# Rounded parts and remainders in the second layer's weighted sum of values, remainders by GpSimd, next scores ahead of it

## The chip, the cores and the metric

The kernel runs on one core of one Trainium2 chip. A core has five engines that run their own instruction streams and meet at semaphores: TensorE (PE, matrix products into PSUM; its weight loads are shown as PEld), VectorE (DVE), ScalarE (ACT), GpSimd (POOL) and SyncE (SP, which here issues transfers). The metric is the time of one execution on the device in microseconds (us). Each kernel was run several times and the median counts.

## What is computed

A trunk of two decoder layers over 256 tokens of 2048 values, in float32. Layer 0 has stick-breaking attention, layer 1 sparse attention, in which each query takes the 64 best of the admissible keys by an index score; both are followed by a gated MLP with a short convolution. The change touches the second layer's attention, the last two of these lines, for 16 query heads in 4 groups that share keys and values:

```python
s = jnp.einsum('btgrd,btkgd->btgrk', qg, k_sel).astype(jnp.float32) * attn_scale
s = jnp.where(valid[:, :, None, None, :], s, -jnp.inf)
p = jax.nn.softmax(s, axis=-1)
o = jnp.einsum('btgrk,btkgd->btgrd', p.astype(v.dtype), v_sel)
...
return out @ w_o
```

The kernel gathers nothing: it adds a mask (selm) to the scores of all 256 keys, so that the keys not chosen get weight zero.

## The kernel before

Weights stream from memory in 771 pieces of 128 x 1024 numbers through a ring of four buffers (raw). For every piece ScalarE makes the rounded part (w_hi, type float32r, line 276) and VectorE the remainder raw - w_hi (w_lo, line 716). TensorE multiplies w_hi with the rounded parts and remainders of the activations side by side (512 columns) and w_lo with the rounded parts (256 columns). So a product in near full precision is made of three single-pass products. float32 operands without such a split go through TensorE at full precision, in more passes.

The order of work is written out by hand, engine by engine. A function block1 on each engine stands for one group of four pieces, e = 0 to 3, of the second layer's input projection; the small steps of attention hang on these e. The 16 heads are worked in 8 pairs, t = 0 to 7. Of a pair t, TensorE does scores(t) (queries by keys, added to the mask that ScalarE has seeded in PSUM banks 6 and 7 by seed_scores), VectorE maxes(t), ScalarE exps(t), VectorE normalise(t), TensorE transposes(t) of the 128 x 768 weights back into banks 6 and 7 behind piece e = 2, ScalarE prt_copy(t) to SBUF (prt, line 610) and then the seed for the next pair's scores (line 597), and TensorE values(t) behind piece e = 3: prt by v_cur, the values of the group, in full precision, with 512 and 256 columns. Behind it stands scores(t+1). ScalarE's out_hi(t) (line 617) and VectorE's out_lo(t) (line 1141) write the result as rounded part and remainder to att, and only then is att_ready raised. scores and values also wait for qr (VectorE, line 1052), the next queries.

Blocks 13 to 18 hold transposes and values of pairs 0 to 5, each with scores of the next pair. The last two pairs hang on the first group of the output projection (out_groups with l1_tail and l1_head; 8 pieces, e = 0 to 7): transposes(6) behind piece 1, values(6) and scores(7) behind piece 2, transposes(7) behind piece 4, values(7) behind piece 5. Piece e of this group multiplies the tiles of pair e, and wo1_ready(e) makes TensorE wait for att_ready of pair e. On ScalarE and VectorE each tail step stands behind the split of piece e + 4, which waits until TensorE has used piece e.

GpSimd fills three buffers at the start and issues three stores at the end of the second layer.

Of the kernel before, what the change touches and what calls it, by code (L numbers as in the profile page):

```python
# [81 lines left out]
def build(nc, x_in, w_all, vecs_in, consts_in, out):  # L82
    with ExitStack() as ctx:
# [3 lines left out]
        def sem(name):  # L87
            return ctx.enter_context(nc.semaphore(name))
# [41 lines left out]
        v_all = sb("v_all", [P, 2, 512], F32, l1)  # L130
        v_cur = sb("v_cur", [P, 2, P], F32, l1)
        k_all = sb("k_all", [P, KVH, T], F32, l1)
# [8 lines left out]
        score = sb("score", [P, 384], F32, l1)  # L141
        work = sb("work", [P, 384], F32, l1)
        cum = sb("cum", [P, 384], F32, l1)
        ones = sb("ones", [P, 256], F32, l1)
# [3 lines left out]
        cmask2 = sb("cmask2", [P, 384], F32, l1)  # L148
        tki = sb("tki", [P, 1, T], F32, l1)
        pr = sb("pr", [P, 2, 384], F32, l1)  # L150
        prt = sb("prt", [P, 2, 384], F32, l1)
        mx = sb("mx", [P, 2, 2], F32, l1)
# [37 lines left out]

        v1_ready, vcur_ready = sem("v1_ready"), sem("vcur_ready")
        tables_ready = sem("tables_ready")
# [8 lines left out]
        s_ready, mx_ready, nm_ready, p_ready, rc_ready, pn_ready = (sem(n) for n in ("s_ready", "mx_ready", "nm_ready", "p_ready", "rc_ready", "pn_ready"))  # L201
        tr_ready, pt_ready, av_ready = sem("tr_ready"), sem("pt_ready"), sem("av_ready")

# [13 lines left out]
        def f32(ap):  # L217
            return ap.bitcast(F32)

        def gain(m, tile):  # L220
# [34 lines left out]
        @block.gpsimd  # L255
        def _(pool):
            pool.memset(part[:, 0:2, :], 0.0).then_inc(warm_set, 1)
            pool.memset(upad[:, :, 0:2], 0.0).then_inc(pads_zero, 1)
            pool.memset(seed[:, 0:Z1], 0.0).then_inc(seed_zero, 1)

            for g in range(3):
                pool.wait_ge(x_ready, 12 + g + 1)
                pool.dma_start(out[:, 4 * g:4 * g + 4, :], xres[:, 4 * g:4 * g + 4, :]).then_inc(stored, 16)
            pool.wait_ge(stored, 48)
# [3 lines left out]
        def _(act):  # L268
# [339 lines left out]
            def prt_copy(t):  # L608
                act.wait_ge(tr_ready, t + 1)
                act.copy(prt[:, :, :], psum[:, 6:8, 0:384]).then_inc(pt_ready, 1)  # L610
                if not isinstance(t, int) or t < PAIRS - 1:
                    act.wait_ge(pt_ready, t + 1)
                    seed_scores()
# [5 lines left out]
            def set_v(g):  # L619

                act.copy(v_cur[:, :, :], v_all[:, :, bass.ds(g * P, P)]).then_inc(vcur_ready, 1)

# [67 lines left out]
            def l1_tail(e):  # L690
                if e == 1:
                    norm_scale(2, 10)
                    prt_copy(6)
                if e == 2:
                    out_hi(6)
                if e == 4:
                    prt_copy(7)
                if e == 5:
                    out_hi(7)
# [5 lines left out]
        def _(dve):  # L705
# [552 lines left out]
            def l1_tail(e):  # L1258
                if e == 0:
                    rope_prev(18, "q", 10, ("sin",))  # L1260
                if e == 2:
                    out_lo(6)
                if e == 5:
                    out_lo(7)
# [6 lines left out]
        def _(pe):  # L1271
# [294 lines left out]
            def values(t, n_v):  # L1566
                pe.wait_ge(pt_ready, t + 1)
                pe.wait_ge(vcur_ready, n_v)
                pe.wait_ge(att_ready, PAIRS + t)
                o = psum[:, 4, :].rearrange("p (h t) -> p h t", h=2)  # L1570
                mm(o, v_cur[:, 0, :], prt[:, :, 0:T], True)
                mm(o[:, :, P:T], v_cur[:, 1, :], prt[:, :, T:384]).then_inc(av_ready, 1)

            def block1(B, i, per, par, prev_nh, prev_nb, t_log, t_score, g_score, t_tr, n_v, base):
# [8 lines left out]
                for e in range(4):  # L1583
                    if index:
                        proj_index(base + e, i, per, 2 * par, 4 * e, e == 0)
                    else:
                        proj(base + e, i, per, 2 * par, xg, 4, 4 * e, 256, e == 0)
                    if e == 1 and prev_nb is not None:
                        mean_squares(prev_nh, prev_nb)
                    if e == 2 and isinstance(B, int) and B == 2:  # L1590
                        turn_wi()
                    if e == 2 and t_tr is not None:
                        transposes(t_tr)
                    if e == 3:
                        if t_log is not None:
                            logits(t_log)
                        if t_tr is not None:
                            values(t_tr, n_v)
                        if t_score is not None:
                            scores(t_score, g_score)  # L1600

# [29 lines left out]
            def l1_tail(e):  # L1631
                if e == 1:
                    mean_squares(2, 10)
                    transposes(6)
                if e == 2:
                    values(6, 4)
                    scores(7, 3)
                if e == 4:
                    transposes(7)
                if e == 5:  # L1640
                    values(7, 4)
# [88 lines left out]
```

## Time and profile before

| | |
|---|---|
| median of 3 runs | 2219.75 us |
| lowest and highest | 2219.74 and 2220.39 us |
| profiled execution | 2219.86 us |
| its span, first to last instruction | 2218.1 us |
| busy share: TensorE, VectorE, ScalarE, GpSimd | 100, 67, 53, 0% |
| granted clock of TensorE | 1.00 |

The profile shows one execution. The 2219.86 us contain the span and some 1.8 us around it. TensorE is busy all the time, so a timeline of its starts shows what each step costs; matmuls overlap, so the distance from one start to the next counts and not the duration printed, which reaches into the next. For the other engines a row in brackets says how long they sat idle and who ended it.

### The profile page before, as it was taken

To read this page: it belongs to the slowest core of one execution; us is meant where nothing else is said; L and a number is where in the kernel's file an instruction comes from. 1 tells how busy PE (TensorE), PEld (TensorE's weight loads), DVE (VectorE), ACT (ScalarE), POOL (GpSimd) and SP (SyncE) were. 2 spreads that over 40 slices of the span, in tenths; PEclk is the share of its full clock that TensorE was granted. 3 is DMA by queue.
4 is the path that set the end of the run, shared out by engine and by line. 5 is a ranking of instruction groups with operands and counts; after the bars stand their busy time and mean duration, and the time that the engine had idled before them with its cause. 6 is when DMAs were issued, how large, how long until landed. Compare 5 with 4: busy or idle time off the path is not lost. (4 is left out here: it accounts for less than half of the span.)

```text
span 2218.1 us, 35419 instructions
## 1 busy us (share of the span) xinstructions
PE 2211.4 (100%) x12790; PEld 1947.8 (88%) x12790; DVE 1494.5 (67%) x1774; ACT 1177.1 (53%) x1409; POOL 3.0 (0%) x10
## 2 busy tenths in 40 slices
PE   9999999999999999999999999999999999999999
PEld 8888898888888888888899888888888888888888
DVE  7666556677777777555578888667777777774444
ACT  7565555555555555444455466555555555553332
POOL 0000000000000000000000000000000000000000
PEclk9999999999999999999999999999999999999999
DMA  7555545555565555555566544455565656565654
GB/s 270 168 170 173 171 162 180 195 184 193 185 196 182 191 187 194 192 190 190 190 206 198 178 156 141 161 183 189 180 199 179 198 180 199 180 199 199 200 197 136
DMA packets 113686, 411.51 MB, mean 186 GB/s; under 512 B 12752, under 2 KB 13392, under 8 KB 113616
## 3 DMA queue, kind: packets, MB, share of 16 engines
q1 hardware_dynamic: 112608, 406.96, 55.9%
q10 hardware_dynamic: 576, 1.97, 0.2%
q0 software_dynamic: 432, 1.57, 0.2%
q8 instruction: 53, 0.87, 0.2%
q14 instruction: 17, 0.14, 0.0%
HBM read 408.36 MB, written 2.10 MB: 185 GB/s over the span
## 5 line engine op out<-in xcount | busy, mean ns | idle before, releaser
L716 DVE TENSOR_TENSOR w_lo<-raw,w_hi 128x1024 fp32r<-128x1024 f32 x769 | 935.2, 1224 | 670.9 <-ACT w_hi L276 665.1
L1273 PE MATMUL psum<-xg,w_hi 128*128 128x512 f32 (+1 forms) x3936 | 1358.5, 391 | 1.2 <-DVE xg L727 0.9
L276 ACT CAST w_hi<-raw 128x1024 fp32r<-128x1024 f32 x770 | 803.0, 1049 | 767.6 <-PE psum L1273 764.8
L1273 PE MATMUL psum<-xg,w_lo 128*128 128x256 f32 (+1 forms) x3920 | 1089.4, 278 | 0.0
L1273 PEld LDWEIGHTS psum<-xg,w_hi 128*128 128x128 f32 x3936 | 735.8, 187 | 156.6 <-issue 3.3
L1273 PEld LDWEIGHTS psum<-xg,w_lo 128*128 128x128 f32 x3920 | 741.2, 189 | 2.7 <-issue 2.2
L1273 PE MATMUL psum<-hid,w_hi 128*128 128x512 f32 x1408 | 488.2, 391 | 0.0
L1273 PE MATMUL psum<-hid,w_lo 128*128 128x256 f32 x1408 | 394.2, 280 | 0.0
L1273 PEld LDWEIGHTS psum<-hid,w_hi 128*128 128x128 f32 x1408 | 263.3, 187 | 57.7
L1273 PEld LDWEIGHTS psum<-hid,w_lo 128*128 128x128 f32 x1408 | 266.1, 189 | 0.0
L1273 PE MATMUL psum<-att,w_hi 128*128 128x512 f32 x512 | 178.8, 393 | 0.0
L976 DVE SCALAR_TENSOR_TENSOR conv<-upad,vecs,conv 128x256 f32<-128x256 f32 x352 | 147.0, 480 | 6.4
L1273 PE MATMUL psum<-att,w_lo 128*128 128x256 f32 x512 | 143.3, 280 | 0.0
L535 ACT ACTIVATE conv<-upad,vecs 128x256 f32<-128x256 f32 x176 | 91.6, 592 | 47.8 <-DVE upad L971 47.8
L1273 PEld LDWEIGHTS psum<-att,w_hi 128*128 128x128 f32 x512 | 95.8, 187 | 20.9
L1273 PE MATMUL psum<-w_hi,xg 128*128 128x512 f32 (+1 forms) x384 | 105.4, 357 | 0.0
L1273 PEld LDWEIGHTS psum<-att,w_lo 128*128 128x128 f32 x512 | 96.8, 189 | 0.1
L1273 PEld LDWEIGHTS psum<-w_hi,xg 128*128 128x128 f32 x384 | 68.3, 189 | 9.9
L1273 PE MATMUL psum<-w_lo,xg 128*128 128x512 f32 (+1 forms) x192 | 67.9, 354 | 0.0
L540 ACT ACTIVATE gates<-conv 128x1024 f32<-128x1024 f32 x22 | 23.4, 1062 | 72.4 <-DVE conv L976 72.4
L543 ACT CAST hid<-gates 128x1024 f32 x22 | 23.2, 1055 | 66.6 <-DVE gates L982 66.6
L971 DVE TENSOR_TENSOR upad<-part,rs 128x1024 f32<-128x1024 f32 x44 | 54.1, 1229 | 1.5
(166 smaller groups left out, 888.4 us busy)
## 6 DMA issues: line engine op xcount, KB each, us to landing
raw<-w_all SPq DMA_DIRECT2D x770, 512.0 KB, 3.4
xres<-x_in SPq DMA_DIRECT2D x3, 512.0 KB, 9.5
cst<-consts_in ACTq DMA_DIRECT2D x2, 768.0 KB, 6.0
out_t<-xres POOLq DMA_DIRECT2D x3, 512.0 KB, 3.7
raw<-w_all SPq DMA_DIRECT2D x2, 256.0 KB, 3.5
xres<-x_in SPq DMA_DIRECT2D x2, 256.0 KB, 4.5
out_t<-xres SPq DMA_DIRECT2D x4, 128.0 KB, 1.8
vecs<-vecs_in ACTq DMA_DIRECT2D x1, 354.0 KB, 7.9
```

The costliest lines, as they stand in the source:

```text
L276: act.copy(w_hi[:, c % RING, :], raw[:, c % RING, :]).then_inc(hi_ready, 1)
L535: last = act.activation(conv[:, k, :], upad[:, k, 0:T], ACT.Identity, scale=conv_scalars(layer, i, val, k, 0), bias=conv_scalars(layer, i, ...
L540: act.activation(gates[:, :, :], conv[:, :, :], ACT.Silu).then_inc(silu_ready, 1)
L543: act.copy(hid[:, bass.ds(4 * i, 4), 0:T], gates[:, :, :]).then_inc(h_hi, 1)
L716: dve.tensor_tensor(w_lo[:, c % RING, :], raw[:, c % RING, :], f32(w_hi[:, c % RING, :]), ALU.subtract).then_inc(lo_ready, 1)
L971: dve.tensor_tensor(upad[:, :, 2:T + 2], part[:, :, :], over_heads(rs[:, 0:T], 4), ALU.mult).then_inc(up_scaled, 1)
L976: last = dve.scalar_tensor_tensor(out=conv[:, k, :], in0=upad[:, k, j:j + T], scalar=conv_scalars(layer, i, val, k, j), in1=conv[:, k, :], ...
L1273: return pe.matmul(o, lhsT, rhs, start=start, stop=True, skip_group_check=True)
```

## The change

values(t) takes rounded parts and remainders. ScalarE copies the transposed weights twice, once in float32 (prt32) and once rounded (prt[:, 0]), and then raises pt_hi; GpSimd subtracts the one from the other (prt[:, 1]) and raises pt_ready. v_cur is made likewise, rounded by ScalarE, its remainder by GpSimd. TensorE makes three single-pass pairs of products in place of one pair in full precision. scores(t+1) stands ahead of values(t) everywhere. values(7), out_hi(7) and out_lo(7) move from behind piece 5 to behind piece 6. The seed waits for pt_hi. The buffers work, cum and tki of the key selection now lie in prt32.

```diff
@@ -257,6 +257,14 @@
+            for t in range(PAIRS):
+                if t % 2 == 0:
+                    g = t // 2
+                    pool.wait_ge(vcur_hi, g + 1)
+                    pool.tensor_tensor(v_cur[:, 1, :, :], v_all[:, :, g * P:(g + 1) * P], f32(v_cur[:, 0, :, :]), ALU.subtract).then_inc(vcur_ready, 1)
+                pool.wait_ge(pt_hi, t + 1)
+                pool.tensor_tensor(prt[:, 1, :, :], prt32[:, :, :], f32(prt[:, 0, :, :]), ALU.subtract).then_inc(pt_ready, 1)
@@ -607,9 +615,10 @@
             def prt_copy(t):
                 act.wait_ge(tr_ready, t + 1)
-                act.copy(prt[:, :, :], psum[:, 6:8, 0:384]).then_inc(pt_ready, 1)
+                act.copy(prt32[:, :, :], psum[:, 6:8, 0:384])
+                act.copy(prt[:, 0, :, :], psum[:, 6:8, 0:384]).then_inc(pt_hi, 1)
                 if not isinstance(t, int) or t < PAIRS - 1:
-                    act.wait_ge(pt_ready, t + 1)
+                    act.wait_ge(pt_hi, t + 1)
                     seed_scores()
@@ -618,7 +627,7 @@
-                act.copy(v_cur[:, :, :], v_all[:, :, bass.ds(g * P, P)]).then_inc(vcur_ready, 1)
+                act.copy(v_cur[:, 0, :, :], v_all[:, :, bass.ds(g * P, P)]).then_inc(vcur_hi, 1)
@@ -695,7 +704,7 @@
                 if e == 4:
                     prt_copy(7)
-                if e == 5:
+                if e == 6:
                     out_hi(7)
@@ -1260,7 +1269,7 @@
-                if e == 5:
+                if e == 6:
                     out_lo(7)
@@ -1568,8 +1577,11 @@
                 o = psum[:, 4, :].rearrange("p (h t) -> p h t", h=2)
-                mm(o, v_cur[:, 0, :], prt[:, :, 0:T], True)
-                mm(o[:, :, P:T], v_cur[:, 1, :], prt[:, :, T:384]).then_inc(av_ready, 1)
+                for hl in range(2):
+                    mm(o, v_cur[:, 0, 0, :], prt[:, hl, :, 0:T], hl == 0)
+                    mm(o[:, :, P:T], v_cur[:, 0, 1, :], prt[:, hl, :, T:384])
+                mm(o, v_cur[:, 1, 0, :], prt[:, 0, :, 0:T])
+                mm(o[:, :, P:T], v_cur[:, 1, 1, :], prt[:, 0, :, T:384]).then_inc(av_ready, 1)
@@ -1594,10 +1606,10 @@
+                        if t_score is not None:
+                            scores(t_score, g_score)
                         if t_tr is not None:
                             values(t_tr, n_v)
-                        if t_score is not None:
-                            scores(t_score, g_score)
@@ -1633,11 +1645,11 @@
                 if e == 2:
+                    scores(7, 3)
                     values(6, 4)
-                    scores(7, 3)
                 if e == 4:
                     transposes(7)
-                if e == 5:
+                if e == 6:
                     values(7, 4)
```

On TensorE, the end of a block with values and scores, before:

```order
L1273 MATMUL psum<-xg,w_lo 128x256
L1569 REGISTER_ALU [waits vcur_ready,pt_ready]
L1273 MATMUL psum<-prt,v_cur 128x512 [waits att_ready]
L1273 MATMUL psum<-prt,v_cur 128x2x128
L1550 REGISTER_ALU
L1551 REGISTER_ALU [waits qr_ready]
L1273 ISA [waits s_seeded]
L1273 MATMUL psum<-k_all,qr 128x128
L1273 MATMUL psum<-k_all,qr 128x256
```

The same place after:

```order
L1559 REGISTER_ALU
L1560 REGISTER_ALU [waits qr_ready]
L1282 ISA [waits s_seeded]
L1282 MATMUL psum<-k_all,qr 128x128
L1282 MATMUL psum<-k_all,qr 128x256
...
L1578 REGISTER_ALU [waits vcur_ready,pt_ready]
L1282 MATMUL psum<-prt,v_cur 128x512 [waits att_ready]
L1282 MATMUL psum<-prt,v_cur 128x2x128
```

The wait for the seed (s_seeded) now comes straight behind the piece, and the wait for the remainders (pt_ready) behind the scores.

On ScalarE, the same block, the split of piece e = 2 and what follows it, before:

```order
L276 CAST w_hi<-raw 128x1024 [waits piece_used]
L610 COPY prt<-psum 128x768 [waits tr_ready]
L597 COPY psum<-selm 128x2x384 [waits pt_ready]
L275 REGISTER_ALU [waits raw_full2]
L276 CAST w_hi<-raw 128x1024 [waits piece_used]
```

And after:

```order
L284 CAST w_hi<-raw 128x1024 [waits piece_used]
L618 COPY prt<-psum 128x768 [waits tr_ready]
L619 CAST prt<-psum 128x768
L605 COPY psum<-selm 128x2x384 [waits pt_hi]
L283 REGISTER_ALU [waits raw_full2]
L284 CAST w_hi<-raw 128x1024 [waits piece_used]
```

One 768-wide instruction more stands between the transposed weights and the seed.

On TensorE in the output projection's first group, at values(7), before (the last matmuls of piece 5, values, the first of piece 6):

```order
L1273 MATMUL psum<-att,w_hi 128x512
L1273 MATMUL psum<-att,w_lo 128x256
L1273 MATMUL psum<-prt,v_cur 128x512 [waits att_ready,vcur_ready,pt_ready]
L1273 MATMUL psum<-prt,v_cur 128x2x128
L1273 MATMUL psum<-att,w_hi 128x512 [waits lo_ready,att_ready]
```

After, with the last matmuls of piece 6, values (three such pairs in all) and then the first of piece 7:

```order
L1282 MATMUL psum<-att,w_hi 128x512
L1282 MATMUL psum<-att,w_lo 128x256
L1282 MATMUL psum<-prt,v_cur 128x512 [waits att_ready,vcur_ready,pt_ready]
L1282 MATMUL psum<-prt,v_cur 128x2x128
...
L1282 MATMUL psum<-att,w_hi 128x512 [waits lo_ready,att_ready]
```

The matmul behind values(7) that waits for att_ready is now that of piece 7, which needs the tiles of pair 7 itself.

## Rows read from the trace of the kernel before

**Rows 1.** The page, part 1; span and clock; longest wait of TensorE (total, times, longest).
```profile
PE 2211.4 (100%) x12790; PEld 1947.8 (88%) x12790; DVE 1494.5 (67%) x1774; ACT 1177.1 (53%) x1409; POOL 3.0 (0%) x10
...
core 0: 2218.1 us, clock 1.000
...
PE psum L1273 <- POOL part L257: 1.3, 1, 1.3
```
**Rows 2.** Timeline, TensorE, block 14: start, us, instruction; transposes(1), piece, values(1), scores(2).
```profile
1318.75 0.82 PE L1562 MATMUL psum<-cst,pr 128*128 128x128 f32 x6
1319.32 0.48 PE L1273 MATMUL psum<-xg,w_hi 128*128 128x512 f32 x1
...
1320.10 0.40 PE L1273 MATMUL psum<-xg,w_hi 128*128 128x512 f32 x1
1320.33 0.28 PE L1273 MATMUL psum<-xg,w_lo 128*128 128x256 f32 x1
1320.45 0.40 PE L1273 MATMUL psum<-xg,w_hi 128*128 128x512 f32 x1
...
1322.22 1.45 PE L1273 MATMUL psum<-prt,v_cur 128*128 128x512 f32 x4
1323.51 1.47 PE L1273 MATMUL psum<-k_all,qr 128*128 x8
1324.63 0.58 PE L1273 MATMUL psum<-xg,w_hi 128*128 128x512 f32 x1
1325.05 0.27 PE L1273 MATMUL psum<-xg,w_lo 128*128 128x256 f32 x1
```
**Rows 3.** Timeline, ScalarE, the same block.
```profile
1319.90 0.80 ACT L610 COPY prt<-psum 128x768 f32<-128x768 f32 x1
1320.72 0.80 ACT L597 COPY psum<-selm 128x768 f32<-128x768 f32 x1
1322.42 1.04 ACT L276 CAST w_hi<-raw 128x1024 fp32r<-128x1024 f32 x1 [0.89 <-PE psum L1273]
```
**Rows 4.** Timeline, VectorE, the same block.
```profile
1321.23 1.22 DVE L716 TENSOR_TENSOR w_lo<-raw,w_hi 128x1024 fp32r<-128x1024 f32 x1
1323.50 1.23 DVE L716 TENSOR_TENSOR w_lo<-raw,w_hi 128x1024 fp32r<-128x1024 f32 x1 [1.05 <-ACT w_hi L276]
```
**Rows 5.** First layer: ScalarE timeline, VectorE group; GpSimd groups (busy, mean ns).
```profile
63.35 0.84 ACT L349 CAST aw_hl<-aw 128x768 fp32r<-128x768 f32 x1
64.09 0.80 ACT L351 COPY psum<-seed 128x768 f32<-128x768 f32 x1
...
L814 DVE TENSOR_TENSOR aw_hl<-aw,aw_hl 128x768 fp32r<-128x768 f32 x7 | 6.7, 955 | 1.1 <-ACT aw_hl L349 1.1
...
L259 POOL MEMSET seed<- 128x512 f32 x1 | 0.5, 524 | 0.0
L1723 POOL MEMSET const-float32-1.0<- 128x1 f32 x1 | 0.1, 98 | 0.0
```
**Rows 6.** Timeline, TensorE, tail: piece 2; transposes(7); values(7) and piece 6.
```profile
1392.91 0.47 PE L1273 MATMUL psum<-att,w_hi 128*128 128x512 f32 x1
...
1403.92 0.82 PE L1562 MATMUL psum<-cst,pr 128*128 128x128 f32 x6
...
1407.40 1.45 PE L1273 MATMUL psum<-prt,v_cur 128*128 128x512 f32 x4
1408.50 0.59 PE L1273 MATMUL psum<-att,w_hi 128*128 128x512 f32 x1
1408.92 0.28 PE L1273 MATMUL psum<-att,w_lo 128*128 128x256 f32 x1
```
**Rows 7.** Timeline, ScalarE, tail: prt_copy(6), seed; split, out_hi(7).
```profile
1393.93 0.79 ACT L610 COPY prt<-psum 128x768 f32<-128x768 f32 x1
1394.75 0.80 ACT L597 COPY psum<-selm 128x768 f32<-128x768 f32 x1
...
1407.65 1.04 ACT L276 CAST w_hi<-raw 128x1024 fp32r<-128x1024 f32 x1 [1.73 <-PE psum L1273]
1408.89 0.59 ACT L617 CAST att<-psum 128x512 fp32r<-128x512 f32 x1 [0.19 <-PE psum L1273]
```
**Rows 8.** Timeline, VectorE, tail: qr, splits, out_lo(6), normalise(7), split, out_lo(7).
```profile
1395.28 0.69 DVE L1052 TENSOR_TENSOR qr<-ra,rsn 128x512 f32<-128x512 f32 x1
1395.89 2.44 DVE L716 TENSOR_TENSOR w_lo<-raw,w_hi 128x1024 fp32r<-128x1024 f32 x2
1398.24 0.68 DVE L1141 TENSOR_TENSOR att<-psum,att 128x512 fp32r<-128x512 f32 x1
...
1402.07 1.01 DVE L1135 TENSOR_SCALAR pr<-pr,rc 128x128 f32<-128x128 f32 x4
...
1408.73 1.22 DVE L716 TENSOR_TENSOR w_lo<-raw,w_hi 128x1024 fp32r<-128x1024 f32 x1 [2.25 <-ACT w_hi L276]
1409.87 0.68 DVE L1141 TENSOR_TENSOR att<-psum,att 128x512 fp32r<-128x512 f32 x1
```

More of the change, by code:

```diff
@@ L130, in build @@
         v_all = sb("v_all", [P, 2, 512], F32, l1)
-        v_cur = sb("v_cur", [P, 2, P], F32, l1)
+        v_cur = sb("v_cur", [P, 2, 2, P], F32R, l1)
         k_all = sb("k_all", [P, KVH, T], F32, l1)
@@ L141, in build @@
         score = sb("score", [P, 384], F32, l1)
-        work = sb("work", [P, 384], F32, l1)
-        cum = sb("cum", [P, 384], F32, l1)
         ones = sb("ones", [P, 256], F32, l1)
@@ L148, in build @@
         cmask2 = sb("cmask2", [P, 384], F32, l1)
-        tki = sb("tki", [P, 1, T], F32, l1)
         pr = sb("pr", [P, 2, 384], F32, l1)
-        prt = sb("prt", [P, 2, 384], F32, l1)
+        prt32 = sb("prt32", [P, 2, 384], F32, l1)
+        prt = sb("prt", [P, 2, 2, 384], F32R, l1)
         mx = sb("mx", [P, 2, 2], F32, l1)
@@ L189, in build @@
         att_hi, att_ready = sem("att_hi"), sem("att_ready")
-        v1_ready, vcur_ready = sem("v1_ready"), sem("vcur_ready")
+        v1_ready, vcur_hi, vcur_ready = sem("v1_ready"), sem("vcur_hi"), sem("vcur_ready")
         tables_ready = sem("tables_ready")
@@ L201, in build @@
         s_ready, mx_ready, nm_ready, p_ready, rc_ready, pn_ready = (sem(n) for n in ("s_ready", "mx_ready", "nm_ready", "p_ready", "rc_ready", "pn_ready"))
-        tr_ready, pt_ready, av_ready = sem("tr_ready"), sem("pt_ready"), sem("av_ready")
+        tr_ready, pt_hi, pt_ready, av_ready = sem("tr_ready"), sem("pt_hi"), sem("pt_ready"), sem("av_ready")
         wg = w_all.rearrange("n p k -> p n k")
@@ L218, in f32 @@
             return ap.bitcast(F32)
+        work, cum, tki = prt32[:, 0, :], prt32[:, 1, :], prt32[:, 0:1, 0:T]
         def gain(m, tile):
```

## The prediction, made before the kernel after was run

> **What bounds the kernel now.** The page's first part and the granted clock come first: TensorE is busy 100% of the span, at full clock throughout, VectorE 67%, ScalarE 53%, GpSimd not at all [rows 1]. A microsecond counts only where it lengthens or shortens TensorE's own row of work, so the change is read off TensorE's timeline at the eight places where a weighted sum of values is computed, here called values(0) to values(7). All times are starts from the timeline of one execution, whose matmul ends are modelled; I use start-to-start distances.
>
> Call P the first matmul of the weight piece that stands between transposes(1) and values(1): P = 1319.32 [rows 2]. The piece takes until P+2.90, values(1) 1.29 us (1322.22 to 1323.51), scores(2) 1.12 us (to 1324.63). The first matmul behind these full-precision ones occupies 0.42 us until the next start, where the same form elsewhere takes 0.23: 0.19 us, one weight load, is exposed there [rows 2]. Nothing else waits. values(0) to values(5) stand in six such blocks; values(6) has scores(7) behind it, values(7) stands alone.
>
> **TensorE's work.** A full-precision pair of 512 and 256 columns costs 1.29 us. In rounded form one pair costs 0.35 (1320.10 to 1320.45, or 1322.22 less 1319.32 over eight pairs with the first a little long) [rows 2]. Three pairs are 1.04. In the new order scores come first, the 0.19 falls at the head of values, and the following piece starts without it: 1.12 + 0.19 + 1.04 = 2.35 against 1.29 + 1.12 + 0.19 = 2.60. Gain 0.25. At values(7), 1.10 + 0.19 [rows 6] becomes 1.04: 0.25 too. **Eight times 0.25: -2.0 us.**
>
> **ScalarE's second copy and the scores put ahead.** ScalarE takes the transposed weights at P+0.58 and seeds the scores' banks from P+1.40 to P+2.20 [rows 3]. Now scores need that seed at P+2.90, where they had 1.29 us more. The second copy adds about 0.74, the distance between two 768-wide ScalarE instructions in a row (63.35 to 64.09) [rows 5]. The seed ends at P+2.94, and since the wait also exposes the scores' weight load (0.19) and a hand-over (0.05), scores start at P+3.15. **Six times 0.25: +1.5 us.** ScalarE's own next instruction stands at P+3.10 after 0.89 us idle [rows 3], so nothing behind the copy moves. In the last group ScalarE comes later: the piece starts at 1392.91, the copy at +1.02, the seed ends at +2.64 [rows 6, 7], now +3.38; scores(7) start at +3.60 and not +2.86: **+0.74 us.**
>
> **GpSimd's subtraction, the unknown term.** The rounded weights are out at P + 0.58 + 0.71 + 0.80 = P+2.09. Values could start at 3.15 + 1.12 + 0.19 = P+4.46, so the remainders must be there at P+4.22: GpSimd has 2.1 us. No row shows GpSimd with an operand to read. Its fills take 0.524 us for 512 columns and 0.098 for one [rows 5], 0.83 ns a column for one stream. For 768 columns one stream gives 0.74 us, two 1.37, and three (two reads, one write, nothing overlapped) 2.0. VectorE does it in 0.955 [rows 5]. I take 1.7, midway between two and three streams: two reads and a write on an engine that shows one stream at 0.83 ns a column, while VectorE, overlapping all three, needs 1.24. When does it start? VectorE runs its 1024-wide subtraction from P+1.91 to P+3.13, then idles 1.05 us [rows 4]. If both engines can read at once: done at P+3.85, no wait. If GpSimd has to let VectorE end: 3.13 + 1.7 = P+4.83, and values wait 0.6. Ends: -0 (one stream, 3.87 even from the late start) and 0.9 (three streams from the late start). It cannot be below zero, since nothing in the term shortens TensorE's row. I take the late start: the spare time of 0.4 us in the early case is used up by any hand-over, while VectorE is inside such an instruction at P+2.1 in every block. **Six times 0.6: +3.6 us.** VectorE's next conversion (P+4.18) is held to P+4.83 likewise, but the next block begins 0.6 later, so its phase stays.
>
> The Trainium skill bears on this. "SBUF — State Buffer", section "Who interferes with whom", says that a VectorE instruction with two SBUF inputs and a GpSimd instruction that reads SBUF exclude each other for their whole length, the first in going first. "GPSIMD Engine Reference", section 3.1, gives 2.6 cycles at 1.2 GHz for each element of such an operation: an estimate of 1.66 us here. By these the wait would be 0.56 us, without the exclusion none. No row of before can show either.
>
> **The tail.** values(6): the rounded weights are out at 1392.91 + 2.53; VectorE is in its 0.69 us multiply until +3.06 and then in two conversions until +5.42 [rows 8]. If GpSimd comes in between, it ends at +4.76, and values(6) start +0.1 late; behind both conversions it would be 2.4. I take **+0.1**. Then ScalarE's and VectorE's writing of values(6) comes late: before, VectorE's att subtraction starts at +5.33 and the weights of pair 7 are normalised at 1403.08 [rows 8], 0.84 before transposes(7) at 1403.92 [rows 6]. Now values(6) end at +6.0, ScalarE's cast follows at about +6.15 to +6.75, VectorE's subtraction at +6.76, 1.43 later; TensorE has slipped 0.5 only. 1.43 - 0.50 - 0.84 is 0.1 over, with an exposed load 0.3; with the held conversions another 0.3. **+0.6 us.** (0.3 of it belongs to GpSimd.)
>
> **One piece later for values(7).** Before, they stand between pieces 5 and 6 of the output projection. Piece 7 multiplies the very tiles that they produce. From the end of piece 5 (1407.40): ScalarE's conversion of the next weights from +0.25, its cast of the result from +1.49, VectorE's conversion from +1.33 to +2.55, its subtraction done at +3.15 [rows 6, 7, 8]. Piece 6 covered that (values(7) 1.10, piece 2.78: 3.9, so 0.7 to spare). Now values(7) stand behind piece 6. The chain is the same, since VectorE's conversion and not the values holds it: done at +3.15, the first matmul of piece 7 at +3.40 with hand-over and load, while TensorE is free at +1.04. **+2.36 us.** The cover, a piece of 2.78 us, is gone and nothing takes its place. The piece gained ahead of values(7) is not needed: remainders are ready about 1408.6 against 1410.2.
>
> The four small value subtractions (256 wide) have over 8 us before their first use; cost nothing, likewise the renamed buffers.
>
> **Sum:** -2.0 + 1.5 + 0.74 + 3.6 + 0.1 + 0.6 + 2.36 = +6.9 us. The profiled execution took 2219.86 us (span 2218.1), 0.1 over the median of three, so about 2226.8.
>
> **Rivals.**
> B, GpSimd is in time: it reads beside VectorE, or is faster than I take it. The 3.6, the 0.1 and 0.3 of the 0.6 go: +2.9, 2222.8. That is no measurable slowdown; it decides at an end of the subtraction before P+4.22. For it speaks that 2.1 us are more than two streams need. Chance 0.27.
> C, the stalls at the seed and at piece 7 are not there either, as they come from sums of 0.2 us hand-overs: only the -2.0, 2217.9. Against it stands the 2.36, where the cover misses by more than 2 us. 0.03.
> D, GpSimd loses to VectorE's back-to-back conversions: in block 0, where they run to P+3.85, and behind both in the tail, with pair 7 following: with three streams 2.9 + 5.4 + 0.7 + 4.8 = 13.8, thus 2233.7. Or TensorE's idle time of over 2 us ahead of piece 7 takes its clock from 2.4 to 1.2 GHz for a stretch: in this trace the level never falls, and TensorE's longest wait is 1.3 us [rows 1]. 0.08.
> E, rounded matmuls from these buffers cost more than a single pass, or what else I overlooked: 0.02.
>
> **The numbers.** The forecast case has 0.60: 2225 to 2231. With its neighbours the range goes from 2221.8 (B less 1 us of errors in the tail) to 2232.5. A measurement of this kernel can tell 0.2%, 4.4 us, from no change. B and C lie within it: 0.29 with a sliver of the forecast's low end. Slower 0.69. Faster by 4.4 us has no mechanism: 0.02.
>
> **What would show it.** In TensorE's timeline of after: scores at P+3.15 and not P+2.90; the first value matmul at P+5.05 (A) or P+4.46 (B); six value matmuls in 1.04 us; a gap of 2.4 us ahead of the last piece of the first output group. In GpSimd's rows: a subtraction of 1.7 us that begins when VectorE's conversion ends, and VectorE's next conversion held. Wrong would be: GpSimd's rows begin at P+2.1 and end before P+4.2, or a gap ahead of piece 7 under 1 us.

## The result

The changed kernel takes 2229.94 us in the median of five runs (2228.6 to 2230.65), the kernel before 2219.75 (2219.31 to 2220.39): 1.0046 times as long, 95% interval 1.0035 to 1.0056, or 10.2 us more. The profiled execution took 2230.65 us with a span of 2228.9; the spans differ by 10.8 us.

The page's first part and the span's clock answer to [rows 1]: GpSimd now works 24.5 us, and the clock is no longer 1.000.

```profile
PE 2216.9 (99%) x12806; PEld 1950.0 (87%) x12806; DVE 1501.3 (67%) x1774; ACT 1183.2 (53%) x1417; POOL 24.5 (1%) x22
...
core 0: 2228.9 us, clock 0.999
```

TensorE's waits from 1300 us on after the change (engine and line waited for: total us, times, longest). The kernel before has none there; its waits, like the other ones after the change, lie ahead of 1200 us:

```profile
PE psum L1282 <- DVE att L1150: 2.0, 1, 2.0
PE psum L1282 <- DVE qr L1061: 1.7, 1, 1.7
PE psum L1282 <- POOL prt L267: 1.3, 4, 0.4
PE psum L1282 <- ACT psum L605: 0.5, 1, 0.5
```

The last one is scores(7) waiting for the seed. They come to 5.5 us. The list leaves out pieces of idle time that a modelled matmul end covers, so the cost is better read from starts.

**A usual block.** TensorE's timeline of block 15 after the change (start, length, operation) answers to [rows 2] one block on: the piece's start P = 1336.83, scores(3), values(2), the next piece.

```profile
1336.83 0.48 PE L1282 MATMUL psum<-xg,w_hi 128*128 128x512 f32 x1
...
1339.88 1.57 PE L1282 MATMUL psum<-k_all,qr 128*128 x8
1341.87 1.32 PE L1282 MATMUL psum<-prt,v_cur 128*128 128x512 f32 x6 [0.41 <-POOL prt L267]
1343.03 0.39 PE L1282 MATMUL psum<-xg,w_hi 128*128 128x512 f32 x1
```

ScalarE's timeline there has the rounded cast, as [rows 3] had the copy:

```profile
1338.10 0.81 ACT L619 CAST prt<-psum 128x768 fp32r<-128x768 f32 x1
```

GpSimd's has the subtraction:

```profile
1338.99 2.66 POOL L267 TENSOR_TENSOR prt<-prt 128x768 fp32r<-128x768 f32 x1 [9.24 <-ACT prt L619]
```

And VectorE's the two conversions of [rows 4]:

```profile
1338.75 1.22 DVE L725 TENSOR_TENSOR w_lo<-raw,w_hi 128x1024 fp32r<-128x1024 f32 x1
1341.01 1.71 DVE L725 TENSOR_TENSOR w_lo<-raw,w_hi 128x1024 fp32r<-128x1024 f32 x1 [1.04 <-ACT w_hi L284]
```

GpSimd is asked at P+2.16 and shows 2.66 us, of which the first 0.98 lie inside VectorE's conversion (until P+3.14). It ends at P+4.82. VectorE's next conversion is asked at P+4.18 and shows 1.71 us in place of 1.23: it ends 1.07 after GpSimd. Each is stretched by about its overlap with the other: GpSimd by 0.83 over the 1.83 us that it takes alone (overlap 0.98), VectorE by 0.48 (overlap 0.64). Scores start at P+3.05, values at P+5.04 and the next piece at P+6.20, where 5.31 + 0.19 = 5.50 stood before: 0.70 us more.

**Block 14.** Here GpSimd came first. P = 1319.84. GpSimd's timeline, then VectorE's, then TensorE's, all after the change:

```profile
1321.99 1.83 POOL L267 TENSOR_TENSOR prt<-prt 128x768 fp32r<-128x768 f32 x1 [13.29 <-ACT prt L619]
```

```profile
1322.08 2.29 DVE L1061 TENSOR_TENSOR qr<-ra,rsn 128x512 f32<-128x512 f32 x1
```

```profile
1324.61 1.57 PE L1282 MATMUL psum<-k_all,qr 128*128 x8 [1.70 <-DVE qr L1061]
...
1327.07 0.39 PE L1282 MATMUL psum<-xg,w_hi 128*128 128x512 f32 x1
```

VectorE's query multiply, a 0.69 us instruction before, began 0.09 us after GpSimd and lasted 2.29. Scores need its result and started at P+4.77. This block lost 1.73 us.

**Piece 7.** values(7) begin at 1415.81. VectorE's timeline has the remainder of their result at its end:

```profile
1417.14 1.22 DVE L725 TENSOR_TENSOR w_lo<-raw,w_hi 128x1024 fp32r<-128x1024 f32 x1 [1.60 <-ACT w_hi L284]
1418.29 0.68 DVE L1150 TENSOR_TENSOR att<-psum,att 128x512 fp32r<-128x512 f32 x1
```

TensorE's has the first matmuls of piece 7, and two of those behind:

```profile
1419.03 0.50 PE L1282 MATMUL psum<-att,w_hi 128*128 128x512 f32 x1 [2.00 <-DVE att L1150]
...
1421.00 0.63 PE L1282 MATMUL psum<-att,w_hi 128*128 128x512 f32 x1
...
1421.64 0.63 PE L1282 MATMUL psum<-att,w_hi 128*128 128x512 f32 x1
```

Before, in [rows 6, 8], the piece followed without a break. A pair takes 0.64 us and not 0.35 between about 1420 and 1423.4. A view by stretches (TensorE busy, weight loads, VectorE, ScalarE, GpSimd, granted clock, DMA share, GB/s) shows the clock of that time:

```profile
1416.00:1419.00 3.00, 1.03 (x6) 0.61 (x5) 1.83 (x2) 1.58 (x2) 0.00 (x0) 1.00 0.55 175
1419.00:1424.00 5.00, 4.97 (x19) 4.25 (x20) 0.00 (x0) 0.26 (x1) 0.00 (x0) 0.66 0.30 105
1424.00:1430.00 6.00, 6.00 (x35) 5.20 (x35) 4.72 (x4) 4.28 (x7) 0.00 (x0) 1.00 0.27 87
```

A mean of 0.66 over five microseconds is some 3.4 us at the lower of the two levels, 1.2 GHz, and the rest at 2.4.

**The account of the 10.8 us**, from the same marks in both traces: 0.2 before the attention's blocks; 0.3 + 1.7 + 0.7 + 0.6 + 0.6 + 0.6 = 4.5 in blocks 13 to 18; 0.5 at scores(7) and values(6); 0.3 from there to piece 5; 2.1 at values(7) and piece 7; 1.6 for the clock; 1.3 in the three further groups of the output projection (22.61 us each against 22.19, see the end); 0.3 in all that follows, nearly all of it at the same slower pace.

### The profile page after: what moved, and what is told of

Its sections match the earlier page's. It is cut to its first block and busy times, and to the rows that moved or that the text cites. A ratio compares the mean times of both kernels' runs of the same rounds, so it can differ in the third digit from the quotient of the medians.

```text
span 2228.9 us, 35473 instructions
## 1 busy us (share of the span) xinstructions
PE 2216.9 (99%) x12806; PEld 1950.0 (87%) x12806; DVE 1501.3 (67%) x1774; ACT 1183.2 (53%) x1417; POOL 24.5 (1%) x22
## 3 DMA queue, kind: packets, MB, share of 16 engines
q10 hardware_dynamic: 576, 1.97, 0.2%
```

## The experiments

Medians are to be compared with 2229.94 for the changed kernel and 2219.75 to 2219.99 for the one before, which ran beside each of them. Ratios are to that one.

### values(7) back behind piece 5

```diff
-                if e == 6:
+                if e == 5:
                     out_hi(7)
...
-                if e == 6:
+                if e == 5:
                     out_lo(7)
...
-                if e == 6:
+                if e == 5:
                     values(7, 4)
```

> The changed kernel with values(7), out_hi(7) and out_lo(7) back behind piece 5 of the output projection. Theory (piece 7 waited 2.0 us for pair 7's result, and the 1.6 us at half clock behind it came from that idle time): both go, but values(7) now wait for GpSimd's remainders, which came 1.18 us after the end of piece 5 in the changed kernel (1412.07 + 1.85 + 0.24 against 1412.98). Sum -2.2 - 1.6 + 1.2 = -2.6 us: 2227.3. No wait ahead of piece 7, no stretch at half clock. Rival (the half clock has another cause, or any wait of 1 us brings it): the clock still falls, 2229 or more. Rival 2 (the piece-7 wait was not what it costs but was covered later): no change, 2229.9.

2226.22 us (1.0028, 1.0017 to 1.0038), 3.7 less than the changed kernel; 2.6 were expected. The wait for att and the stretch at half clock are gone, and GpSimd is waited for once more: values(7) started 3.88 us behind the start of piece 5, 0.98 late. TensorE's waits of this kernel:

```profile
PE psum L1282 <- POOL prt L267: 2.3, 5, 0.8
```

This idle time of 0.8 us left the clock at 1.00. Between the two profiled executions the order by itself makes 1.2 us, where 1.0 was expected (2.2 less 1.2), and the low stretch 1.6. The groups behind took 22.19 us and not 22.61, which makes another 1.5 us with what follows them and was in no expectation.

### Remainders by VectorE

```diff
+            def prt_lo(t):
+                dve.wait_ge(pt_hi, t + 1)
+                dve.tensor_tensor(prt[:, 1, :, :], prt32[:, :, :], f32(prt[:, 0, :, :]), ALU.subtract).then_inc(pt_ready, 1)
...
+                    if e == 3 and t_soft is not None:
+                        prt_lo(t_soft)
                     split(base + e + RING, i, per)
...
+                if e in (1, 4):
+                    prt_lo(6 + e // 4)
```

GpSimd's subtraction for prt is taken out; values(7) stay behind piece 6.

> The changed kernel with the remainders of the transposed weights made by VectorE instead of GpSimd, in the place where VectorE idled 1.04 us ahead of the split of piece e = 3 (tail: behind the split of pieces 1 and 4). Theory (GpSimd and VectorE hold each other up): the waits of values for GpSimd and the late qr of block 14 go, the six blocks lose 0.3, 1.7, 0.7, 0.6, 0.6, 0.6 us less, 4.5 together: 2225.4. VectorE's 0.96 us fits its idle time. Rival (VectorE is nearly full in these blocks, so that its own 0.96 us comes back as late queries or late conversions): gain under 2 us, 2228 to 2230. Piece 7 still waits 2.0 us and the clock falls in both.

2225.37 us (1.0025, 1.0015 to 1.0035): 4.6 less, 4.5 expected. That they agree so well is in part luck: the granted clock of a whole execution is 0.999 in four of the changed kernel's five and in one of this one's nine, so the medians compare a kernel that mostly has the low stretch with one that mostly has not. The two profiled executions both have it. In them, from block 13 to piece 2 of the output projection, the changed kernel loses 4.6 us on the one before and this one 0.8: GpSimd's part there is 3.8 us. VectorE has room for it, as its timeline of block 15 shows (P = 1335.35): conversion, remainder, conversion, with 0.20 us idle left of the 1.05.

```profile
1337.21 1.22 DVE L723 TENSOR_TENSOR w_lo<-raw,w_hi 128x1024 fp32r<-128x1024 f32 x1
1338.34 0.95 DVE L1147 TENSOR_TENSOR prt<-prt 128x768 fp32r<-128x768 f32 x1
1339.49 1.23 DVE L723 TENSOR_TENSOR w_lo<-raw,w_hi 128x1024 fp32r<-128x1024 f32 x1 [0.20 <-ACT w_hi L282]
```

Values now start at P+4.28, before the P+4.46 of the forecast, and the next piece at P+5.52, where it stood at 5.50 before. Blocks 14 to 18 lose 0.1 us in all; block 13 keeps 0.65, of which 0.3 are a wait for VectorE's remainder. The wait of 2.0 us ahead of piece 7 stays, and in the profiled execution a low stretch behind it that costs 1.4 us.

### Both

> Both edits of the two kernels before it. Theory: -4.5 for GpSimd, -2.2 and -1.6 for piece 7 and the clock, +0.4 since values(7) wait shortly for VectorE: about 2222, still 2 us over the kernel before, of which 1.5 + 0.7 are the seed's waits less the 2.0 that the single-pass products save. Rival (slow pace of products behind the waits is a cost of its own): up to 1.3 us less again, if it goes with the waits, 2220.7.

2223.18 us (1.0014, 1.0004 to 1.0023). The sum came out 1.2 higher than expected and the rival's 2220.7 is off by 2.5. With neither GpSimd nor the wait at piece 7, the kernel is still 3.3 us over the one before, in the profiled spans too. Of these, 0.8 stand in the blocks, nearly all in block 13, 1.0 at scores(7) and values(6), where the seed comes late and values start late behind the scores, and 1.5 in the pace of the later groups. That pace is the slow one here, with the long waits gone, so it does not go with them.

### Filling the gap ahead of piece 7

```diff
                 if e == 6:
                     values(7, 4)
+                    for n in range(6):
+                        mm(psum[:, 5, :], xg[:, 0, 0:P], xg[:, 1, :], True)
```

These products go to a bank that nobody reads.

> The changed kernel with six 512-wide rounded matmuls into an unused PSUM bank behind values(7), 1.3 us of the 2.0 us in which TensorE waits for pair 7. Theory (idle time took the clock down): piece 7 begins at the same time, the stretch at half clock is gone or shorter: -1.6 us, 2228.3. Rival (the half clock is not from that gap): unchanged 2229.9. If the filling itself delayed piece 7, its start would show it.

2228.64 us (1.0039), 1.3 less than without them; the profiled spans differ by 1.9, of which 0.3 came before this place. Piece 7 started 3.21 us behind values(7), as before (3.22), after a wait of 0.6 us. The view by stretches, as above, of this kernel:

```profile
1419.00:1424.00 5.00, 5.00 (x30) 4.30 (x29) 1.01 (x1) 1.96 (x2) 0.00 (x0) 1.00 0.34 105
```

Thirty matmuls in the five microseconds in place of 19, all at full clock: with most of the idle time gone, so was the low stretch. The median fits too: the one execution of the changed kernel with a granted clock of 1.000 took 2228.6 us. Is the gap enough for it? Three profiled kernels have the gap of 2.0 us. Remainders by VectorE shows a clock of 0.58 and then 0.85 in two stretches of 3 us behind it. The third is the one with GpSimd's subtraction in halves (below). First its wait, then its stretch behind the gap:

```profile
PE psum L1283 <- DVE att L1151: 2.0, 1, 2.0
```

```profile
1421.00:1424.00 3.00, 3.00 (x19) 2.67 (x18) 0.00 (x0) 0.58 (x1) 0.00 (x0) 1.00 0.43 156
```

The same idle time, full clock, and pairs 0.35 us apart. So the low stretch followed a gap of 2.0 us in two profiled executions of three; none of the other kernels, whose waits from 1300 us on are 1.7 us at most, shows one at this place.

The granted clock of every execution says how often. Measured to three digits, a stretch like this turns 1.000 into 0.999. Of the kernels with the gap, the changed one has 0.999 in 4 executions of 5, remainders by VectorE in 1 of 9, the subtraction in halves in 1 of 10. The ten other kernels tried here have it in 1 of 93, the kernel before in 3 of 86, with one more at 0.949; where in those executions the clock fell, no trace shows. With the gap the low stretch is more frequent, but it is neither certain nor bound to it. With the same gap it is frequent in one kernel and rare in two, so that the five executions of the filled kernel, all at 1.000, make the gap its likely cause and do not prove it. The Trainium skill, "TensorE: Matmul & The Clock Gate", part 1, describes these two levels, given by how busy TensorE was. The traces agree as to the levels, 0.50 and 1.00 of the full clock; that the same gap can go either way is what the runs add.

### The order alone, and the order with the second copy

The kernel before with scores ahead of values:

```diff
+                        if t_score is not None:
+                            scores(t_score, g_score)
                         if t_tr is not None:
                             values(t_tr, n_v)
-                        if t_score is not None:
-                            scores(t_score, g_score)
```

> The kernel before with scores(t+1) ahead of values(t), nothing else: full-precision values, one copy. Theory: the seed is there at P+2.20, the piece ends at P+2.90, so the order alone costs nothing: 2219.8, within 0.3. Rival (the order itself costs, since result and maxima of a pair come later or earlier): 2221 or more.

and with ScalarE's second copy as well:

```diff
+                act.copy(prt2[:, :, :], psum[:, 6:8, 0:384])
                 act.copy(prt[:, :, :], psum[:, 6:8, 0:384]).then_inc(pt_ready, 1)
```

> The same and a second 768-wide copy by ScalarE of the transposed weights ahead of the first, to a buffer nobody reads in the attention. Theory: the seed comes at P+2.94 and scores start 0.16 to 0.25 us late in six blocks, 0.6 late in the tail: +1.6 to +2.2 us over the kernel before, 2221.4 to 2222. Rival (ScalarE's copy is hidden, the late scores of the changed kernel come from VectorE's queries): within 0.3 of the order alone.

2221.02 us (1.0006, 0.9996 to 1.0015) and 2224.13 us (1.0017, 1.0007 to 1.0027). The order alone is not to be told from no change, although its median is 1.0 us higher and stands at the rival's 2221. Its profiled execution, with a span 2.7 us longer than that of the kernel before, has 1.6 of them in the pace of the later groups (22.61 us), 0.35 ahead of block 13, 0.2 in the blocks and 0.6 behind them. In its block 15 scores started at P+2.91 (1338.10 against 1335.19), the next piece at 5.32 + 0.19 as before. The copy costs 3.1 us more, the expectation for it was 1.6 to 2.2; the profiled spans differ by 2.2. In its block 15 scores started at P+3.06 (1338.80 against 1335.74), values another 1.41 later and not 1.30: 0.26 us a block, where I had 0.25. The medians differ by 0.9 more than the spans because the profiled execution of the order alone, 2222.64 us, is the longest of its ten, 1.6 over their median; that of the other is 0.6 over its own. The ten fall into 2220.4 to 2221.1 and 2221.9 to 2222.6, and the slower pace may be what parts them, but only one of them has a trace.

### Values cut in two

The products with the rounded weights come straight behind the piece, then scores, then the product with the remainders; values(7) stand behind piece 5. Remainders by VectorE:

```diff
                         if t_tr is not None:
-                            values(t_tr, n_v)
+                            values_hi(t_tr, n_v)
+                        if t_score is not None:
+                            scores(t_score, g_score)
+                        if t_tr is not None:
+                            values_lo(t_tr)
```

> Values cut in two: the two pairs of products with the rounded weights stand straight behind the piece, then scores, then the pair with the remainders; remainders by VectorE, values(7) behind piece 5. Theory: the 0.70 us of the first two pairs cover the seed's wait (P+2.94 against P+3.60), scores and these cover the remainders (about P+4.1 against P+4.7): no wait is left, only the saving of 0.25 us eight times: 2217.8 to 2218.3, below the kernel before. Rival (VectorE's extra 0.96 us a block comes back elsewhere): 2220 to 2223.

and by GpSimd:

> The same cut of values, with GpSimd making the remainders. Theory: remainders at about P+4.8 (GpSimd behind VectorE's conversion) against P+4.7: waits of 0.1 to 0.3 us in most blocks, and where GpSimd comes in ahead of the query multiply, a block 1.7 us late: 2219.5 to 2222. Rival (no exclusion, waits only from GpSimd's own 1.8 us): P+3.95, no wait, 2218.

2219.4 us (0.9998, 0.9989 to 1.0008) and 2226.04 us (1.0025, 1.0015 to 1.0035). Between these two only the engine of one subtraction differs, and it makes 6.6 us, or 5.5 from block 13 to piece 7 in the profiled executions, ahead of the groups whose pace differs. TensorE's waits in the one with VectorE have nothing new but 0.3 us once:

```profile
PE psum L1288 <- DVE prt L1147: 0.3, 1, 0.3
```

Where nothing waits, in its blocks 16 to 18, values and scores together take 2.36 us (0.70, 1.12 and 0.54), against 2.60 before and a forecast of 2.35.

TensorE's waits in the one with GpSimd show that it is not GpSimd's result that is late, but VectorE's queries, four times:

```profile
PE psum L1282 <- DVE qr L1061: 5.0, 4, 1.4
...
PE psum L1282 <- POOL prt L267: 0.2, 1, 0.2
```

My expectation for GpSimd (2219.5 to 2222) took that for a rare case. It is a race between the rounded cast on ScalarE, which releases GpSimd at P+2.16 in each block, and the multiply on VectorE, and the kernel loses it in every second block. In blocks 14, 16 and 18 GpSimd is asked 0.64, 0.23 and 0.39 us before the multiply starts; in 13, 15 and 17 it is 0.13, 0.41 and 0.40 behind. The multiply stands at P+2.03 in block 13, P+2.80 in block 14 and P+1.74 in block 15: a late block holds TensorE up more than VectorE, and in the next one VectorE is in time. The version with VectorE came out 0.6 us lower than the kernel before, within what the runs can tell; the expected 2217.8 to 2218.3 are missed by 1.1. Its profiled execution is slower than the median, 2220.86 us. It is 1.0 us ahead of the kernel before from block 13 to piece 2, where six times 0.25 were expected, then loses 0.6 at scores(7) and values(6), with the wait shown, and 1.5 by groups at 22.61 us.

### GpSimd that nobody waits for: reading, and writing only

Into the version with VectorE's remainders went a GpSimd subtraction of the same size, from other buffers into one that nobody reads:

```diff
+                pool.wait_ge(pt_hi, t + 1)
+                if t:
+                    pool.wait_ge(gp_done, t)
+                pool.tensor_tensor(upad[:, 0:3, 2:T + 2], k_all[:, 0:3, :], k_all[:, 1:4, :], ALU.subtract).then_inc(gp_done, 1)
```

> The kernel with values cut in two and VectorE's remainders, and in it a GpSimd subtraction of the same size (768 wide, two SBUF operands, from k_all to a buffer that nobody reads), released with the rounded weights as the remainders' one was; no engine waits for it inside the attention. Theory (a GpSimd instruction that reads SBUF and a VectorE one with two SBUF operands exclude each other): VectorE's query multiply, remainder or conversion is held up to 1.8 us in each block, and TensorE waits for queries or remainders: 3 to 9 us over the same kernel without it, 2222.5 to 2228.5. Rival (GpSimd's harm was only that values waited for it): no change, 2219.4.

and in its place two fills:

```diff
+                pool.wait_ge(pt_hi, t + 1)
+                for n in range(2):
+                    if t or n:
+                        pool.wait_ge(gp_done, 2 * t + n)
+                    pool.memset(upad[:, 0:3, 2:T + 2], 0.0).then_inc(gp_done, 1)
```

> The same with two 768-wide fills by GpSimd in place of the subtraction, about 1.5 us of GpSimd in all at the same moment, which write SBUF and read nothing. Theory (it is the reading that excludes VectorE): no change against the kernel without it, 2219.4 within 0.6. Rival (any GpSimd work in SBUF holds VectorE up): 2 to 7 us slower.

2231.99 us (1.0049, 1.0034 to 1.0064) with the subtraction, 12.6 over the version without it, and 2220.08 us (0.9995, 0.998 to 1.001) with the fills, 0.7 over it where 0.6 was allowed. From block 13 to the end the profiled execution with the fills is as long as the one without them to 0.1 us, the slower groups left out of the latter; its excess stands ahead of block 13, where none of these fills has run. Eight instructions that nobody needs cost more than the whole change did. TensorE's waits in the kernel whose GpSimd reads:

```profile
PE psum L1293 <- DVE prt L1151: 8.3, 7, 1.4
```

GpSimd's timeline in its block 14, and VectorE's:

```profile
1322.71 2.26 POOL L269 TENSOR_TENSOR upad<-k_all 128x768 f32<-128x768 f32 x1 [14.38 <-ACT prt L621]
```

```profile
1323.18 2.87 DVE L727 TENSOR_TENSOR w_lo<-raw,w_hi 128x1024 fp32r<-128x1024 f32 x1
```

The same two in the kernel whose GpSimd only writes:

```profile
1322.58 1.55 POOL L270 MEMSET upad<- 128x768 f32 x2 [13.54 <-ACT prt L622]
```

```profile
1322.96 1.22 DVE L728 TENSOR_TENSOR w_lo<-raw,w_hi 128x1024 fp32r<-128x1024 f32 x1
```

Reading, GpSimd stretches the conversion from 1.22 to 2.87 us. Writing at the same moment, it leaves it at 1.22. My range for the reading one (3 to 9 us) was too low: I had priced a hold in some blocks, and it fell in all six of them, 1.1 to 1.4 us of waiting each, because VectorE's remainder queues behind the held conversion. That is the rule of the Trainium skill's "SBUF — State Buffer", section "Who interferes with whom", in both its halves: reading excludes, writing does not, and the traces agree. The two kernels differ also in the kind of instruction, a subtraction and two fills; a GpSimd instruction of another kind that reads was not run.

### The subtraction in halves

```diff
-                pool.tensor_tensor(prt[:, 1, :, :], prt32[:, :, :], f32(prt[:, 0, :, :]), ALU.subtract).then_inc(pt_ready, 1)
+                pool.tensor_tensor(prt[:, 1, 0, :], prt32[:, 0, :], f32(prt[:, 0, 0, :]), ALU.subtract)
+                pool.tensor_tensor(prt[:, 1, 1, :], prt32[:, 1, :], f32(prt[:, 0, 1, :]), ALU.subtract).then_inc(pt_ready, 1)
```

> The changed kernel with GpSimd's subtraction in two halves of 384. Theory (the exclusion lasts one instruction): VectorE gets in between the halves, so the query multiply in block 14 is held about 0.9 us instead of 1.7, but where VectorE's conversion of 1.2 us comes between, the remainders come later: -0.8 in block 14, up to +1.2 in blocks where both compete. Sum open, 2228 to 2233; VectorE's longest stretched instruction falls from 2.3 to about 1.5 us. Rival (exclusion lasts until GpSimd is done with all it has): 2230, the stretch of 2.3 us stays.

2230.49 us (1.0041, 1.0025 to 1.0056), no gain. GpSimd's timeline of blocks 13 and 14:

```profile
1306.13 1.41 POOL L267 TENSOR_TENSOR prt<-prt 128x384 fp32r<-128x384 f32 x1 [7.59 <-ACT prt L620]
1307.51 1.97 POOL L268 TENSOR_TENSOR prt<-prt 128x384 fp32r<-128x384 f32 x1
1322.76 1.84 POOL L267 TENSOR_TENSOR prt<-prt 128x384 fp32r<-128x384 f32 x1 [13.29 <-ACT prt L620]
1324.57 0.99 POOL L268 TENSOR_TENSOR prt<-prt 128x384 fp32r<-128x384 f32 x1
```

A half alone takes 0.99 us. In block 13 VectorE came in between the two (the second half shows 1.97), so the exclusion lasts one instruction. In block 14 the cast came later and GpSimd was second, so VectorE's multiply took 0.69 us there and not 2.29. But the late half makes the remainders late: 4.3 us of waiting for GpSimd in seven places, the longest 1.1, against 1.3 in four. What one side gains the other pays. The profiled span is 1.9 us shorter than that of the changed kernel, by what it lacks: the low clock (1.6) and the slower pace of groups (1.5), less 1.3 of longer waits. It is one of two executions at 2228.8; the other eight lie between 2230.3 and 2230.7, and seven of them have a granted clock of 1.000.

### The last version

As the kernel with values cut in two and VectorE's remainders, those of pair 6 one step earlier:

```diff
                 if e == 1:
                     rope_prev(18, "q", 10, (1,))
+                    prt_lo(6)
```

> Values cut in two with VectorE's remainders, those of pair 6 made ahead of the split behind piece 1 and not behind it. Theory: TensorE's wait of 0.33 us for the remainders of pair 6 goes: 0.3 to 0.5 us less than 2219.4, so 2219.0, below the kernel before by 0.5 to 1 us, not to be told from it if the pace of the output projection (22.2 or 22.6 us a group) falls out differently. Rival: the delayed conversion is waited for, 2219.6 or more.

2220.47 us (0.9995, 0.9981 to 1.0009). 2219.0 was expected, and it fell on the rival's side. The wait of 0.33 us is gone, and 0.30 us ahead of transposes(7) came in its place, for pair 7's weights. No version beats the kernel before beyond what the runs can tell.

## Why the prediction was right, point by point

The forecast was 2226.8 with 2221.8 to 2232.5, slower with a chance of 0.69. The measured 2229.94 lie within, 3.1 above the forecast, and the loss is 4.6 thousandths. The spans of the profiled executions differ by 10.8 us where the sum had 6.9. Of the 3.9 missing, 1.6 are the clock, 1.5 the pace of the later work, 0.2 stand ahead of the blocks and 0.6 in the terms that were forecast: 1.0 too little in the six blocks, 0.4 too much behind them. That these small errors partly cancel is luck.

- **The subtraction's price and start: right.** 1.7 us forecast; 1.68 behind VectorE's end in block 15, and 1.83 and 1.85 where GpSimd had its way. End at P+4.83 forecast, P+4.82 measured; values at P+5.07 and P+5.04. Rival B, a subtraction that is in time, is out in the blocks from 15 on, where it ends at P+4.7 to P+4.8, and so is its sum: remainders by VectorE, without the exclusion, gave back 3.8 us in the blocks.
- **What was missed in it:** GpSimd getting in ahead of VectorE's query multiply. I had the late start in every block and looked only at who waits for GpSimd, not at what it holds up when it comes first. In block 14 it ran from P+2.15 to P+3.98, which the prediction had named as a sign that it was wrong, and the block cost 1.7 us in place of 0.6; block 13, where the late conversion hid behind TensorE's work, 0.3. Six blocks: 4.5 against 3.6.
- **The seed's wait: right in size,** 0.15 us at the start of scores (P+3.05; the forecast's terms add up to P+3.18, and it took 3.15) and about 0.1 more to the start of values, tested by the copy alone. **The saving: right in the blocks** too, 0.24 us where nothing waits (2.36 against 2.60, values cut in two). Behind the seed's wait scores and values together take 2.46 us (1401.18 to 1403.64); those are the 0.1 of the wait once more and no second loss. Seed and saving together were forecast at 0 a block; remainders by VectorE show 0.02 in block 15.
- **scores(7), values(6):** next piece at +5.95 in the trace, as in the forecast without its 0.1 for late remainders. GpSimd came in between, as forecast, and TensorE waited for nothing but the seed.
- **transposes(7):** a stall of 0.6 forecast, 0.3 found.
- **Piece 7: right.** VectorE's remainder done 3.16 us behind the start of values(7), forecast 3.15; 2.0 us of idle time.
- **The clock: a rival that happened.** Case D had it, at a chance of under 0.08 with the rest of D; it cost 1.6 us in the profiled execution. The step that failed is that the forecast priced the idle time at its own length alone. 0.999 stands in four of this kernel's five executions, and in two of 19 in the two other kernels with the same gap.
- **The pace of the output projection and what follows it,** 1.5 us in this profile, was in no term.

## What to carry to other kernels

A second engine's help is not free because that engine is idle: if it reads SBUF while VectorE's instructions have two SBUF operands, each holds the other for its whole instruction, and TensorE pays through whichever result stands next in line. A unit of work put one piece later should be followed to its last reader; here the reader was the very next piece, and the gap cost its own 2 us and, in the profiled execution, 1.6 more through the clock. Where a product is split in parts, the parts that are ready can cover the wait for those that are not: that order, with VectorE making the remainders and values(7) back in their place, won back the loss and no more.

## What was not expected of the hardware

- The exclusion goes both ways by whoever is first, and being 0.09 us ahead was enough: 2.66 us for GpSimd behind VectorE's conversion, 2.29 us for a 0.69 us VectorE multiply behind GpSimd.
- The same gap of 2.0 us ahead of piece 7 was followed by the lower clock in two profiled executions and not in a third, and in four of the changed kernel's five executions the granted clock is 0.999. What decides it stays open.
- Groups of the output projection with the same 64 pairs of matmuls and the same waits take 22.19 us in some profiled kernels (before, values(7) early, remainders by VectorE alone, values in two with GpSimd, GpSimd writing, halves) and 22.61 in the others: a pair takes 0.3466 or 0.3533 us from the first matmul of a group to its last. The granted clock is 1.00 in both. It goes with none of the edits, makes 1.3 us in three groups here, and its cause stays open. ScalarE's copies at the end of two groups after the change, 22.61 us apart:

```profile
1424.69 1.01 ACT L308 COPY part<-psum 128x1024 f32<-128x1024 f32 x1
1447.30 1.01 ACT L308 COPY part<-psum 128x1024 f32<-128x1024 f32 x1
```

In the kernel before, the same copies stand at 1415.45 and 1437.64, 22.19 apart.
